# The WKV-7 recurrence of a two-block model: from one chunk solve a pass, head by head, to a pipeline of three solves a pass, both heads in step

## The reference, cut to what matters

```python
def step(state, inp):                     # per head, state is 64 x 64
    r_t, w_t, k_t, v_t, a_t, b_t = inp
    sa = jnp.einsum('bhvk,bhk->bhv', state, a_t)
    state = state * w_t[:, :, None, :] + sa[..., None] * b_t[:, :, None, :] + v_t[..., None] * k_t[:, :, None, :]
    y = jnp.einsum('bhvk,bhk->bhv', state, r_t)
    return state, y
_, y = lax.scan(step, s0, seq, reverse=reverse)
...
y_f, bonus_f = direction(0)
y_b, bonus_b = direction(1)
y = y_f + y_b
```

## Time and profile before

| | |
|---|---|
| median of 3 runs | 2790.9 us (2789.16 to 2795.78) |
| profiled execution, span from first to last instruction | 2791.3 us |
| the loop of the recurrence | 764.0 us to about 1235 us of the span |
| busy over the span | PE 97%, PEld 77%, DVE 50%, ACT 45%, POOL 44% |

### The profile page before, as it was taken

One profiled execution on the slowest core, in us unless ns is written; L12 is line 12 of the kernel. 1 busy time (PEld: TensorE's weight loads), 2 busy tenths in 40 slices (PEclk: granted clock), 3 DMA queues, 4 the chain that ended last, 5 costly groups with the idle time before them and its releaser, 6 DMA issues.

```text
span 2791.3 us, 55493 instructions
## 1 busy us (share of the span) xinstructions
PE 2697.6 (97%) x23340; PEld 2154.4 (77%) x23340; DVE 1402.7 (50%) x2503; ACT 1264.0 (45%) x2292; POOL 1233.6 (44%) x1145
## 2 busy tenths in 40 slices
PE   8999999989999999989999999999999999999999
PEld 6678888867778888777888877587777777788887
DVE  6847885055667777754888022612223333244410
ACT  5754443234666666544444235634444453422221
POOL 5234444546733433325444446054443645544443
PEclk9999999999999999999999999999999999999999
DMA  5112332322300000103332322032222322323222
GB/s 177 42 54 91 93 96 91 94 95 91 90 16 6 8 8 8 36 29 98 91 98 87 96 88 76 12 114 74 76 77 69 100 74 91 98 91 98 89 90 78
DMA packets 67079, 208.64 MB, mean 75 GB/s; under 512 B 14736, under 2 KB 15376, under 8 KB 66448
## 3 DMA queue, kind: packets, MB, share of 16 engines
q1 hardware_dynamic: 63680, 192.96, 22.5%
q0 software_dynamic: 2576, 10.78, 1.1%
q10 hardware_dynamic: 576, 1.35, 0.1%
HBM read 199.69 MB, written 4.19 MB: 73 GB/s over the span
## 4 chain that ended last, share of the span: by engine, by line
PE 88%; DVE 6%; ACT 2%; POOL 2%; issue 2%; DMA 0%; SPq 0%; DVEq 0%; ACTq 0%; POOLq 0%
PE banks L1803 22%; PE banks L1805 22%; PE banks L1804 22%; PE banks L826 6%; PE banks L835 1%; PE banks L1975 1%; PE banks L943 1%; POOL low L321 1%; PE banks L819 1%; PE banks L2037 1%; PE banks L2023 1%; PE banks L892 1%; DVE low L550 1%; PE banks L2012 1%; DVE arena L2842 1%
## 5 line engine op out<-in xcount | busy, mean ns | idle before, releaser
L321 POOL TENSOR_TENSOR low<-arena,high 128x256 fp32r<-128x256 f32 (+3 forms) x817 | 967.7, 1207 | 1149.8 <-ACT high L309 1149.7
L1803 PE MATMUL banks<-high,high 128*128 128x512 f32 (+1 forms) x2728 | 1080.8, 396 | 10.9 <-DVE arena L2706 2.9
L1805 PE MATMUL banks<-high,low 128*128 128x512 f32 (+1 forms) x2728 | 1070.5, 392 | 0.0
L1804 PE MATMUL banks<-low,high 128*128 128x512 f32 (+1 forms) x2728 | 1070.1, 392 | 0.0
L309 ACT ACTIVATE high<-arena 128x1024 fp32r<-128x1024 f32 (+1 forms) x376 | 382.1, 1016 | 799.3 <-PE banks L1805 797.7
L1803 PEld LDWEIGHTS banks<-high,high 128*128 128x128 f32 x2728 | 513.5, 188 | 139.2 <-issue 5.5
L1805 PEld LDWEIGHTS banks<-high,low 128*128 128x128 f32 x2728 | 513.4, 188 | 119.6
L1804 PEld LDWEIGHTS banks<-low,high 128*128 128x128 f32 x2728 | 513.7, 188 | 117.8 <-issue 1.9
L2740 DVE TENSOR_TENSOR arena<-banks,arena 128x512 f32<-128x512 f32 x48 | 33.1, 692 | 424.4 <-PE banks L1805 423.3
L2871 DVE SCALAR_TENSOR_TENSOR arena<-arena 128x511 f32<-128x511 f32 x88 | 237.2, 2695 | 3.1
L826 PE MATMUL banks<-arena 64*64 64x64 f32 x5632 | 200.3, 222 | 17.6 <-ACT arena L1204 10.7
(11 more groups left out here) (319 smaller groups left out, 3079.4 us busy)
## 6 DMA issues: line engine op xcount, KB each, us to landing
arena<-weights SPq DMA_DIRECT2D x301, 512.0 KB, 3.5
arena<-weights SPq DMA_DIRECT2D x48, 448.0 KB, 3.3
arena<-weights SPq DMA_DIRECT2D x28, 256.0 KB, 2.6
arena<-tables POOLq DMA_DIRECT2D x5, 448.0 KB, 3.6
arena<-x_t SPq DMA_DIRECT2D x4, 512.0 KB, 5.8
x_spill<-arena POOLq DMA_DIRECT2D x1, 2048.0 KB, 9.4
arena<-x_spill POOLq DMA_DIRECT2D x1, 2048.0 KB, 8.8
out_t<-arena SPq DMA_DIRECT2D x8, 256.0 KB, 4.1
```

Of the source, the lines that this page charges most:

```text
L321: low = pool.tensor_tensor(lo[:, part], ring[w % RING][:, part], hi[:, part].bitcast(F32), ALU.subtract)
L1803: pe.matmul(dst, hi[:, c], x[0], start=kt == 0, stop=False)
L1804: pe.matmul(dst, hi[:, c], x[1], start=False, stop=False)
L1805: mm = pe.matmul(dst, lo[:, c], x[0], start=False, stop=kt == kts_of[t] - 1)
```

## The change

Three solves are under way in one pass: solve `i` grows, solve `i-1` is merged, and solve `i-2` runs the sequential part. The loop has `ITERS + 2` = 34 passes in place of 33. Both heads share each instruction of ACT, DVE and POOL: one copy of 128x512 in place of two of 128x256, one addition of 128x256 in place of two of 128x128. The additions of U2, U3 and U4 on DVE go; in their place the identity is added to the power (W2 on POOL, W4 and W8 on DVE), and ACT copies the product. PE's `both` goes over q, p and h for every step, and for some steps the halves that it reads or writes are turned for the second head ("turned"). The three buffers of U need room: two of them lie in the first tile of x's place, so that x comes back in two DMAs, the tile of 256 KB only after the last solve, and the low part of one weight piece of `rw_o` is split after the loop. The order of the side pieces changes; DVE's first piece now stands behind the turned masks. The comments in the diff are added for the reader.

```diff
-    INV_PE = ["NT", "A"] + two("S1") + ["S2_0", "U2_0", "S2_1", "U2_1", "S3_0", "U3_0", "S3_1", "U3_1"] + \
-        two("T", "U4", "Q1", "U5", "Q2", "U6")
+    SCORE_PE, MASK_DVE = ["NT", "A"], ["N", "DT", "M", "D"]
+    GROW_PE, GROW_ACT = ["S1", "S2", "S3", "U2", "U3", "U4"], ["S1", "S2", "U2", "U3", "U4"]
+    GROW_DVE, GROW_POOL = ["W4", "W8"], ["U1", "W2"]
+    MERGE_PE, MERGE_ACT, MERGE_DVE = ["Q1", "U5", "Q2", "U6", "T"], ["Q1", "Q2", "T"], ["U5", "U6"]
...
+        def both(into, col, lhs, rhs, rows_in, rows_out):
+            row = {"even": lambda p, h: hf(p), "turned": lambda p, h: hf(p ^ h)}
             for q in range(2):
                 for p in range(2):
                     for h in range(2):
+                        r, to = row[rows_in](p, h), row[rows_out](p, h)
+                        mm = pe.matmul(into[h][to, col + C * q:col + C * q + C], lhs(r, h, q), rhs(r, h, q), start=True, stop=True)
+            return mm
...
+        for i in range(ITERS + 2):                      # PE
+            growing, merging, seq = i < ITERS, 0 < i <= ITERS, i > 1
+            if merging:
+                grow(i - 1, 4)                          # even, even
+            if growing:
+                turned_scores(i)
+            if seq:
+                solve(i - 2, 0)
+            side(i, "state 0")
+            if merging:
+                merge(i - 1, 1)                         # even, turned
+            if growing:
                 scores(i)                               # waits for DT
+            if merging:
+                merged(i - 1, 1)                        # turned, even
             if seq:
+                advance_state(i - 2, 0)
+                second_state(i - 2, 0)
+            if growing:
+                square(i, 1)                            # waits for D; even, even
+            if seq:
+                read_state(i - 2, 1)
+            if merging:
+                merge(i - 1, 2)
+            if growing:
+                square(i, 2)                            # even, turned
+            if seq:
+                solve(i - 2, 1)
+            if merging:
+                merged(i - 1, 2)
+            side(i, "merged")
+            if growing:
+                square(i, 3)                            # turned, even
+            if seq:
+                advance_state(i - 2, 1)
+                second_state(i - 2, 1)
+            if growing:
+                grow(i, 2)                              # even, turned
+            if merging:
+                tokens(i - 1)                           # waits for W8 of solve i
+            if growing:
+                grow(i, 3)                              # turned, even
+            side(i, "grown")
+            if merging:
                 read_state(i - 1, 0)
...
+            if growing:                                 # DVE, one pass
+                mask_turned(i)                          # N 128x512, DT 128x256
+            spread(i, "first")
+            spread(i, "masks")
+            if growing:
+                mask_lanes(i)                           # M 128x768, waits for A
             if seq:
+                new_state(i - 2, 0)
+            if merging:
+                add_merged(i - 1, 5)
+            if growing:
+                mask_diagonal(i)                        # D 128x256
             if seq:
+                add_values(i - 2, 1)
+            spread(i, "state")
+            if merging:
+                add_merged(i - 1, 6)
+            if growing:
+                ga.wait(dve, i, "S2")
+                with_unit(R.P2[:, :, 0, :], R.P4[:, :, 1, :], "W4")
+                gp.wait(dve, i, "S3")
+                with_unit(R.P4[:, :, 0, :], both_j[:, :, 0:P], "W8")
+            spread(i, "powers")
             if seq:
+                new_state(i - 2, 1)
+            spread(i, "last")
+            if merging:
+                add_values(i - 1, 0)
...
+            elif at_ == (3, "powers") and j:            # DVE's side pieces, c = 3
+                y_square(j - 1)
+                y_var(j - 1)
+            elif at_ == (3, "last") and more:
+                r_(j + 1, 1)
+                a_(j + 1, 1)                            # AR1
...
             if c == 0:                                  # POOL, one pass
                 k_sum(j)
+            md.wait(pool, i, "D")
+            gg.inc(pool.tensor_tensor(R.U[i % 3], R.D, eyes, ALU.add), "U1")
+            gg.wait(pool, i, "U1")
+            ga.wait(pool, i, "S1")
+            gg.inc(pool.tensor_tensor(R.D, R.P2[:, :, 1, :].rearrange("p h (q c) -> p h q c", q=2), eyes, ALU.add), "W2")
...
+        mp.wait(pool, ITERS - 1, "U6")
+        split_low(pool, late_piece)
+        pc.wait(pool, 2 * ITERS - 1, "SA")
+        load_back(0, 1)
```

More of the change, by code:

```diff
@@ L780, in side @@
                     od.wait(pe, j - 2, "y")
[L781 to L784, removed]
+                gate(j - 2, bank)
+            elif at_ == (2, "grown") and j < KT:
                 if j >= 2:
@@ L789, in side, with turned_scores @@
                 bonus(j, bank)
-            elif at_ == (3, "masks") and j:
+            elif at_ == (3, "state 0") and j:
                 ba.wait(pe, j, "bon")
                 turn_y(j - 1, "bt", bank)
[L793 to L797, removed]
+        def turned_scores(i):
             j, c = i // TT, i % TT
@@ L818, in scores @@
                         for h in range(2):
-                            mm = pe.matmul(PI[h][hf(p), 256 * q + P * k:256 * q + P * k + P], BK[d][k][hf(h), C * n:C * n + C],
+                            mm = pe.matmul(PJ[h][hf(p), 256 * q + P * k:256 * q + P * k + P], BK[d][k][hf(h), C * n:C * n + C],
                                            AR[d][hf(h), n, :, :].rearrange("p a b -> p (a b)"), start=True, stop=True)
[L821 to L831, removed]
+            sp.inc(mm, "A")
+        def both(into, col, lhs, rhs, rows_in, rows_out):
+            row = {"even": lambda p, h: hf(p), "turned": lambda p, h: hf(p ^ h)}
             for q in range(2):
@@ L877, in merge @@
[L877 to L894 removed]
+                mm = both(PJ, P, m, mt, *way)
@@ new lines, in merge, with merged, tokens @@
+        def merge(i, m):
+            u = lanes_of(R.U[i % 3])
+            if m == 1:
+                ga.wait(pe, i, "U4")
+            else:
+                mb.wait(pe, i, "U5")
+            both(PI, 0, half_of(R.NM[i % 2], m - 1), u, "even", "turned")
+            mp.inc(both(PI, P, u, unit, "even", "turned"), f"Q{m}")
+        def merged(i, m):
+            ma.wait(pe, i, f"Q{m}")
+            mp.inc(both(PI, 2 * P, half_of(R.Q, 1), half_of(R.Q, 0), "turned", "even"), f"U{m + 4}")
+        def tokens(i):
+            j, c = i // TT, i % TT
+            if i + 1 < ITERS:
+                gd.wait(pe, i + 1, "W8")
+            for d in range(2):
+                ch = lane(c, 0, d)[1]
+                for k in range(2):
+                    pe.transpose(PJ[d][:, P * k:P * k + P], R.BK[j % 2][d][k][:, ch * P:(ch + 1) * P], ident)
+            for h in range(2):
+                for q in range(2):
+                    for p in range(2):
+                        mm = pe.matmul(PJ[h][hf(p), 2 * P + C * q:2 * P + C * q + C], R.AM[i % 3][hf(p), h, q, C:2 * C],
+                                       values(i, c, q, p, h), start=True, stop=True)
+            mp.inc(mm, "T")
@@ new lines, in half_merged, with turned, solved, outputs @@
+        def half_merged(i, m):
+            mp.wait(act, i, f"Q{m}")
+            ma.inc(act.activation(pairs(R.Q), both_i[:, :, 0:2 * P], ACT.Copy), f"Q{m}")
+        def turned(i):
+            mp.wait(act, i, "T")
+            ma.inc(act.activation(R.TK[i % 2], both_j[:, :, 0:3 * P], ACT.Copy), "T")
+        def solved(it, q):
+            pc.wait(act, 2 * it + q, "SA")
+            ac.inc(act.activation(R.SA.rearrange("p a b -> p (a b)"), PP[0][:, 0:P], ACT.Copy), "SA")
+        def outputs(it, q):
+            pc.wait(act, 2 * it + q, "Y")
+            for p in range(2):
+                d, ch, n = lane(it % TT, q, p)
+                o_ = act.activation(R.Y[it // TT % 2][d][hf(p), ch, :, :], both_x[hf(p), :, C:2 * C], ACT.Copy)
+            ac.inc(o_, "Y")
@@ L1714, in dve_rwkv @@
         y_var(KT - 1)
-        z_low(KT - 3)
         z_gate(KT - 2, psum[2])
```

603 lines of the change are left out of this document (258 added, 345 removed).

## The result

| | before | changed |
|---|---|---|
| median | 2791.3 us (4 runs, 2789.2 to 2795.8) | 2844.4 us (4 runs, 2841.1 to 2847.9) |
| ratio, 95% interval | | 1.0185 (1.017 to 1.020) |
| profiled execution, span | 2791.3 us | 2843.8 us |
| first NT to last NT | 447.7 us | 481.2 us |
| last NT to the first matmul of `rw_o` | 23.4 us | 41.9 us |

A forecast was written before the change was run, and what follows sets the result against it. PE was taken to bound the kernel, its 1.5 us a pass saving mostly eaten by waits; -5 us from all passes and +8 from clock falls gave +3 to +4, so 2795 us, 8-in-10 range 2769 to 2817.

The forecast's parts named there:

- PE's work: In each loop pass, four-quarter steps save 1.1 us and a single visit for turning operands about 0.4, together 1.5.
- rival (c): Slower, 0.21: first, S1 and U4 queue on one quarter, 25 us (2820); second, clock falls in ordinary passes, up to +30.
- (b): Faster, 0.27: DVE and POOL alternate more kindly, `a_` ends before PE comes to the next NT, no clock fall; 2771.
- (d): PE stays the bound in all passes, 0.07: 50 us gained, less 8 to 10 for the pass added; 2750.
- (a): Likeliest, 0.45: PE's gain eaten by the wait for D and by AR1 (DVE's `a_`); 2795, range 2784 to 2804.
- S1's wait for D: In an ordinary pass PE runs dry at 4.1 us and waits for DVE's diagonal mask: 1.3 us of new idle time.
- In the ordinary passes the new idle 1.3 us leaves about 2.4 of 3.4 busy, ... nothing: PE stays busy enough in ordinary passes that the clock holds: no cost, at the upper bound 30 us.
- seven falls at the joins: Between pairs of heads, PE's idle time behind the fourth pass lowers the clock: 7 x 1.2 = +8 us.
- DVE W8 0.5: In an ordinary pass, W8 on DVE takes 0.5 us, from 9.95 to 10.55, before the tokens; the pass takes 13.5.
- the fourth pass: c = 3 of a pair: DVE and POOL alternate over five POOL operations, `a_` ends at 16.0, pass 16.1 us.
- the 34th pass comes on top: about +2: The last four passes win 1.5 us each, but with the added pass the end costs about 2 us more.
- -5 for the first four passes: Nothing is merged in the first pass or solved in the second: about 52.5 us in place of 57.6.

The follow-up runs named there:

- experiment 3: Changed kernel with S2, S3, U2 and U3 back on 'even' halves for both heads (two quarters of the array, not four): 2857.6 us, ratio 1.0228.
- number 7: Changed kernel with D directly behind M, `k_sum` back behind U1 and `r_` of the next pair one place earlier: 2795.5 us, ratio 1.0003.
- experiment 1: Changed kernel with DVE's diagonal mask D directly behind the lanes' mask M, ahead of new state and U5: 2811.3 us, ratio 1.0061.
- number 6: Changed kernel with its last two passes (drain) altered by four edits on ACT, DVE and PE, loop before them untouched: 2832.7 us, ratio 1.0134.
- experiment 2: Changed kernel with extra unused matmuls where PE stands idle (before S1, at joins, in passes 0, 32, 33): 2828.6 us, ratio 1.0127.
- experiment 11: Changed kernel with one added wait: POOL's `k_a` waits for DVE's W4 in a pair's second and third pass: 2838.4 us, ratio 1.0159.
- number 9: Changed kernel with D early, `k_sum` behind U1, `r_` earlier, altered drain, and unused matmuls in passes 0, 1 and at joins: 2780.8 us, ratio 0.9957.
- experiment 4: Changed kernel with POOL's `k_sum` back behind U1, no longer ahead of the wait for D: 2824.5 us, ratio 1.0114.

## Why the prediction was wrong

The run came out 49 us above the forecast. By the table of stretches: 6 us in the first four passes, 15 in the middle groups' passes even without a fall (7 of them in the fourth), 11 in falls of the clock there (18 against 7), 17 in the last group and drain, 2 behind it, and -1.5 ahead of the loop.

**Right: PE's work.** Four quarters cost 15 to 16 ns an instruction (start to start, the merge and S2), two 29 (S1, and S2 in experiment 3); the block with S2 took 1.36 us against 1.86. By the rule of the Trainium skill that I had weighed ("TensorE: Matmul & The Clock Gate", Part 3) the two would be equal; the trace decides otherwise. In number 7's group at a clock of 1.00 PE is busy for 49.55 us in place of 55.35, 1.45 us less a pass, forecast 1.5. S1, with four instructions in a row on a quarter, kept 29 ns: rival (c)'s first half is refuted. So are (b), which had no wait for AR1, and (d). What came is (a) in both its places, with (c)'s second half and several terms too small on top.

**Right: S1's wait for D.** Dry at 4.1 us and S1 at 5.35 in the working; in the trace (c = 1) PE is dry at 4.2 and S1 starts at 5.6, behind 1.38 us of idle time. I had noted that the second reading of the state and merge 2 stand behind this wait and that it eats the gain. What I didn't ask is what stands ahead of D on DVE without being needed by it: new state and U5. That one order is worth 33 of the 53 us (experiment 1).

**Failed: "In the ordinary passes the new idle 1.3 us leaves about 2.4 of 3.4 busy, ... nothing".** In the 3.4 us ahead of the fall at 912.4 us PE was busy for 1.91, not 2.4: idle time in front of U2 and of the tokens (0.62 and 1.03 us) lies in it, which the sum did not have. In this pass alone POOL has the `hidden_rest` operation of L1403 (1.29 us) ahead of `k_a`; DVE's L1537 (128x8) takes 1.21 us beside it in place of 0.19, and W4 behind it 1.24. In number 6 the same pass had the first meeting but not the second (W4 0.41), took 14.1 us in place of 17.7 and had no fall. So this fall came of a meeting of DVE and POOL as much as of the gap before S1. I named 30 us as the upper bound of this and gave it to rival (c), second half. The forecast was seven falls at the joins, 8 us; twelve falls came, 78.5 us at half clock. By the prices of experiment 2 (0.3 to 0.4 us in the middle groups, a quarter in passes 0 and 1 and the drain) they are worth some 20 to 25 us, an estimate; filling the gaps gave 16 back, net of what the fillers cost. A fall at a join costs 1.4 us (15.9 against 14.5), forecast 1.2: the size was right, the number and places were not.

**Failed: "DVE W8 0.5", and 13.5 us for an ordinary pass.** I let DVE and POOL collide only in the fourth pass. W4, an operation that the change adds with both operands in SBUF, meets `k_a` in the second and third too (1.25 and 0.62 us in place of 0.42), and the tokens wait for W8 behind it. Experiment 11 gives back 6 us, at the edge of the noise, and brings c = 1 to 13.65, near the forecast. c = 2 stays at 13.85; what its last 0.35 us are is not shown.

**Mis-sized: the fourth pass, 16.1 forecast, 17.24 measured.** The alternation with the four `b_k` came as worked out, but `k_sum`, counted as the fifth operation ahead of `a_`, met `a_` itself: "`a_` ends 0.55 later" was 2.10 us. Without it c = 3 is 15.82. Six times 1.14 is 7 us. (The sum 8.2 + 5 x 1.25 + 1.2 is 15.65 and not 15.5, which makes the forecast pass 0.15 longer and no more.)

**Failed: "the 34th pass comes on top: about +2", and -5 for the first four passes.** I priced passes without a growing or a merging solve by PE's work. Passes 0, 1, 32 and 33 are chains: each step waits for the one before on another engine, PE stands idle between and the clock falls (13.7 us of half clock in passes 0 and 1, 20.5 in the drain). The first four passes took 58.9 us in place of 52.5, the last group and drain 18.8 more than before in place of 2: together 23 of the 49 us. With fillers in passes 0 and 1 and the altered loop (number 9) the first four passes do take 52.5. Of the 18.8 us 8 to 14 went with the edits of experiment 6; the rest no run removed.

**Nothing, as forecast:** x's late return and the late split; from `rw_o`'s first matmul to the end +2.1 us, with some 3 us more of half clock in it.

What remains open is the split of the 33 us of experiment 1 between the path itself (31 x 0.95 = 29 us) and falls, the same split for experiment 4, and why a pass has a fall in one group, or in one execution, and none in another.

## What to carry to other kernels

When an edit hands a queue a new order, list for the operation that the busiest engine waits for what is queued ahead of it without being needed; here a new state and one addition in front of D cost 33 us, of 50 that the saved work promised. Price the first and last passes of a deeper pipeline by their chains and not by the busy engine's work, and count every new idle stretch as a possible fall of the clock. A new operation of DVE with both operands in SBUF has to be laid against POOL's queue in every pass, and one wait on POOL can be cheaper than the meeting (6 us here, at the edge of the noise).

## What the runs showed of the hardware that I had not expected

- Half clock costs less than half its length where PE waits for others: in passes 0 and 1 and the drain 31 us less of it gave 7.5 us; in the middle groups 41 us of it were worth an estimated 0.3 to 0.4 us each.
- Where the clock falls differs between executions: 37.5 and 58.0 us at half clock in loops of the same code (experiment 6).
- Neighbouring 64x64 matmuls that share their rows but not their columns run at 16 ns an instruction; over two quarters the same ones take 29 (S2, experiment 3).
- A POOL operation of 1.27 us makes a DVE operation longer by 1.42 (L1554: 0.68 and 2.10 us), by more than its own length, though the DVE operation is recorded as starting first.
